# Row exchange for rotary embedding: matrix products replaced by transfers inside SBUF in two of three mixers

## The reference, cut to what matters

```python
def apply_rope(x, cos, sin):
    half = x.shape[-1] // 2
    x1, x2 = x[..., :half], x[..., half:]
    rot = jnp.concatenate([-x2, x1], axis=-1)
    return x * cos + rot * sin
```

## Time and profile before

| | us |
|---|---|
| median of 3 runs | 1736.95 |
| lowest to highest | 1736.74 to 1737.29 |
| the profiled execution, its own time | 1736.61 |
| its span, first to last instruction | 1735.1 |
| TensorE busy in it | 1628.5 |
| VectorE busy in it | 709.8 |
| ScalarE busy in it | 435.5 |

### The profile page before, as it was taken

One profiled execution on the slowest core, in us unless ns is written; L12 is line 12 of the kernel. 1 busy time (PEld: TensorE's weight loads), 2 busy tenths in 40 slices (PEclk: granted clock), 3 DMA queues, 4 the chain that ended last, 5 costly groups with the idle time before them and its releaser, 6 DMA issues.

```text
span 1735.1 us, 22294 instructions
## 1 busy us (share of the span) xinstructions
PE 1628.5 (94%) x9390; PEld 976.6 (56%) x9390; DVE 709.8 (41%) x1379; ACT 435.5 (25%) x770; POOL 32.6 (2%) x39
## 2 busy tenths in 40 slices
PE   7999999999999999999999988988988898889888
PEld 4786999998799999788222322322222223223222
DVE  3677889884787557695111101101101011101102
ACT  3223643435554445453000000000000000000001
POOL 0100000000000000200100000000000000000000
PEclk9999999999999999999999999999999999989999
DMA  9865388848257454329899999999999999999997
GB/s 389 339 243 218 122 322 328 328 164 345 80 207 273 174 215 157 136 98 360 362 415 431 430 431 430 431 431 429 432 430 430 431 430 430 431 431 431 430 430 301
DMA packets 46034, 577.95 MB, mean 333 GB/s; under 512 B 5200, under 2 KB 6256, under 8 KB 9968
## 3 DMA queue, kind: packets, MB, share of 16 engines
q1 hardware_dynamic: 45936, 576.54, 80.6%
HBM read 575.47 MB, written 1.05 MB: 332 GB/s over the span
## 4 chain that ended last, share of the span: by engine, by line
PE 63%; DMA 32%; DVE 2%; ACT 1%; issue 1%; SPq 1%; ACTq 0%; DVEq 0%
DMA RING_T<-in_w_up 29%; PE P L1338 16%; PE P L554 6%; PE P L947 4%; PE P L949 4%; PE P L948 4%; PE P L966 2%; PE P L965 2%; PE P L964 2%; PE P L563 2%; PE P L1365 2%; DMA RING_T<-in_ada_w 1%; DMA RING_T<-in_w_down 1%; PE P L1112 1%; PE P L1114 1%; PE P L1113 1%
## 5 line engine op out<-in xcount | busy, mean ns | idle before, releaser
L1338 PE MATMUL P<-RING_T,SCR 128*34 128x512 f32 x928 | 439.0, 629 | 83.0 <-DMA RING_T<-in_w_up 83.0
L1339 PE MATMUL P<-RING_T,SCR 128*34 128x512 f32 x960 | 453.8, 629 | 0.0
L1338 PEld LDWEIGHTS P<-RING_T,SCR 128*34 128x34 f32 x928 | 104.7, 117 | 366.6 <-issue 365.6
L2874 DVE TENSOR_TENSOR SCR<-P,SCR 34x512 f32<-34x512 f32 x64 | 44.4, 693 | 543.2 <-ACT SCR L2012 543.2
L1365 PE MATMUL P<-RING_T,SCR 128*34 128x512 f32 x480 | 214.6, 595 | 0.4 <-DMA RING_T<-in_w_down 0.4
L1366 PE MATMUL P<-RING_T,SCR 128*34 128x512 f32 x480 | 214.7, 595 | 0.0
L949 PE MATMUL P<-SCF 128*128 128x256 f32 x640 | 181.1, 283 | 0.0
L947 PE MATMUL P<-SCF 128*128 128x256 f32 x640 | 181.1, 283 | 0.0
L948 PE MATMUL P<-SCF 128*128 128x256 f32 x640 | 181.1, 283 | 0.0
L2012 ACT ACTIVATE SCR<-P 34x512 f32<-34x512 f32 x64 | 37.7, 589 | 570.9 <-PE P L1339 570.9
L1365 PEld LDWEIGHTS P<-RING_T,SCR 128*34 128x34 f32 x480 | 49.9, 111 | 135.7 <-issue 130.9
(11 more groups left out here) (430 smaller groups left out, 2438.1 us busy)
## 6 DMA issues: line engine op xcount, KB each, us to landing
RING_T<-in_w_up SPq DMA_DIRECT2D x58, 2048.0 KB, 21.4
RING_T<-in_w_down SPq DMA_DIRECT2D x57, 2048.0 KB, 17.7
RING_T<-in_w_gate SPq DMA_DIRECT2D x56, 2048.0 KB, 18.2
RING_T<-in_ada_w SPq DMA_DIRECT2D x24, 2048.0 KB, 10.4
RING_T<-in_ffn_w SPq DMA_DIRECT2D x22, 2048.0 KB, 8.7
RING_T<-in_ffn_w SPq DMA_DIRECT2D x22, 1024.0 KB, 6.7
RING_T<-in_ab_w_in SPq DMA_DIRECT2D x7, 2048.0 KB, 14.3
RING_T<-in_w_in SPq DMA_DIRECT2D x6, 2048.0 KB, 7.8
```

Source lines behind the costliest of these rows:

```text
L1338: pe.matmul(u.t[0:CAP, :], xs, wg.v(KC, 512)[:, c, :], start=c == 0, stop=c == KC - 1)
L1339: ins = pe.matmul(u.t[64:64 + CAP, :], xs, wu.v(KC, 512)[:, c, :], start=c == 0, stop=c == KC - 1)
```

## The change

In the first and third mixer, the rotation products of all queries, of the indexer's queries and of the third mixer's keys are gone. In their place ScalarE's queue issues transfers from SBUF to SBUF that exchange the row halves into the unused output buffer (`SW`). A head size of 128 takes two transfers, one of 64 takes four. VectorE multiplies the exchanged rows by the sines in place and adds the cosine part. The sign has moved from the matrix to the sines. The first mixer's keys and its index key are still exchanged on TensorE. In all, 44 transfers are added (8 for `iq`, 4 for the queries, 32 in the third mixer). 4 products of 512 columns and 8 of 272 columns are removed, and with them 4 and 8 uses of PSUM banks. The counts that others wait for on `rope` and `drope` are raised, as a rotation by transfer counts twice. Names of semaphores that nothing uses are dropped, too.

```diff
+def act_swap(nc, k, dst, src, rows, sem):
+
+    for z in range(0, 128, 2 * rows):
+        nc.scalar.dma_start(dst[z:z + rows], src[z + rows:z + 2 * rows]).then_inc(k.sem[sem], 16)
+        nc.scalar.dma_start(dst[z + rows:z + 2 * rows], src[z:z + rows]).then_inc(k.sem[sem], 16)
...
+def dve_swapped(nc, k, dst, sw, tmp, sinv, swap, cos_n, cos_sem, sem, n):
+
+    dve, s = nc.vector, k.sem
+    dve.wait_ge(s[swap[0]], swap[1])
+    dve.wait_ge(s[cos_sem], cos_n)
+    dve.tensor_tensor(sw, sw, sinv, ALU.mult).then_inc(s[sem], 1)
+    dve.wait_ge(s[sem], n)
+    dve.tensor_tensor(dst, sw, tmp, ALU.add).then_inc(s[sem], 1)
...
@@ pe_ab
     chunk("gqk", 1)
-    for j in range(4):
-        pe.wait_ge(P["iq", j].taken, P["iq", j].done)
-    pe_rope(nc, k, "rope_iq0", "rot64", v.IQ[:, 0:2, :])
     chunk("gqk", 2)
     chunk("gqk", 3)
-    pe_rope(nc, k, "rope_iq1", "rot64", v.IQ[:, 2:4, :])
...
-    pe.wait_ge(s["norm"], 2)
-    pe_rope(nc, k, "rope_q0", "rot128", v.QA[:, 0:2, :])
-    pe_rope(nc, k, "rope_q1", "rot128", v.QA[:, 2:4, :])
...
-    pe.wait_ge(s["rope"], 7)
+    pe.wait_ge(s["rope"], 11)
@@ pe_diff
-    chunk("k2", 0)
-    rope("q2", v.Q, 0)
-    rope("q2", v.Q, 1)
-    chunk("k2", 1)
-    rope("q2", v.Q, 2)
-    rope("q2", v.Q, 3)
-    for j in (2, 3):
+    for j in range(4):
         chunk("k2", j)
-        rope("k2", v.K, j - 2)
...
     rows(0)
-    rope("k2", v.K, 2)
-    rope("k2", v.K, 3)
     attend(0)
@@ act_ab
     for j in range(1, 4):
         chunk("iq", j, v.IQ[:, j, :])
+    for j in range(2):
+        act.wait_ge(P["iq", j].taken, P["iq", j].done)
+    act_swap(nc, k, v.SW[:, 0:2, :], v.IQ[:, 0:2, :], 32, "swap0")
     u = P["decay"]
     act_out(nc, u, v.BT.rearrange("p a b -> p (a b)"), u.t[:, :])
+    for j in range(2, 4):
+        act.wait_ge(P["iq", j].taken, P["iq", j].done)
+    act_swap(nc, k, v.SW[:, 2:4, :], v.IQ[:, 2:4, :], 32, "swap1")
...
     for z in range(2):
         act.wait_ge(s["norm"], 1 + z)
+        act_swap(nc, k, v.SW[:, 2 * z:2 * z + 2, :], v.QA[:, 2 * z:2 * z + 2, :], 64, f"swap{2 + z}")
         square(v.norms[z], flat(v.KA)[:, 512 * z:512 * z + 512])
@@ act_diff
+    def swap(name, src, n):
+        u = P[name, n % 4]
+        act.wait_ge(u.taken, u.done)
+        act_swap(nc, k, v.SW[:, n, :], src[:, n % 4, :], 32, f"swap{min(n, 6)}")
+
     for j in range(4):
         chunk("q2", j, v.Q[:, j, :])
         split.upto(NSPLIT + j + 1)
+        swap("q2", v.Q, j)
     for j in range(4):
         chunk("k2", j, v.K[:, j, :])
         split.upto(NSPLIT + j + 5)
+        swap("k2", v.K, 4 + j)
@@ dve_ab, and the same for rope_q0 and rope_q1
-    dve_rope(nc, k, "rope_iq0", v.IQ[:, 0:2, :], tmp(0), s64, 1, "rope", "cosm")
-    dve_rope(nc, k, "rope_iq1", v.IQ[:, 2:4, :], tmp(1), s64, 2, "rope", "cosm")
+    dve_swapped(nc, k, v.IQ[:, 0:2, :], v.SW[:, 0:2, :], tmp(0), s64, ("swap0", 64), 1, "cosm", "rope", 1)
+    dve_swapped(nc, k, v.IQ[:, 2:4, :], v.SW[:, 2:4, :], tmp(1), s64, ("swap1", 64), 2, "cosm", "rope", 3)
@@ dve_diff
-        dve.tensor_tensor(src[:, j, :], u.t[:, 0:L], k.SINR, ALU.mult).then_inc(u.taken, 1)
-        dve.wait_ge(u.taken, u.done)
-        dve.tensor_tensor(src[:, j, :], src[:, j, :], tmp, ALU.add).then_inc(s["drope"], 1)
+        dve_swapped(nc, k, src[:, j, :], v.SW[:, n - 1, :], v.bufs[j % 2][:, 0, 0:L], k.SINR, (sem, by), n, "dcos", "drope", 2 * n - 1)
@@ constants
-                m[o + d % n + h, d] = -1.0
+                m[o + d % n + h, d] = 1.0
```

More of the change, by code:

```diff
@@ L132 @@
 UNIT_HIGH, UNIT_LOW = {"ab": 6, "cd": 3}, {"ab": 6, "cd": 4}
+SWAPPED = [("swap0", 128), ("swap1", 128), ("swap2", 96), ("swap3", 96), ("swap4", 64), ("swap5", 64), ("swap6", 128), ("swap6", 128)]
 SQ = {"mix0": 0, "ffn0": 8, "mix1": 16, "ffn1": 24, "mix2": 32, "ffn2": 40}
@@ L269 @@
     "czeros", "cols", "cond", "ada", "mod", "xr", "sa", "square", "squares", "ln", "rs", "lnsq", "hs", "hn",
-    "angle", "trig", "g1one", "iwt", "gate_a", "gate_d", "decay_a", "decay_d", "cosm", "rope", "qeke", "kdqd", "atzero", "at", "relu", "score",
-    "topk", "state", "ot", "nsq", "norm", "logit", "soft", "softmax", "silu_g", "mix",
+    "swap0", "swap1", "swap2", "swap3", "swap4", "swap5", "swap6",
+    "angle", "trig", "g1one", "gate_a", "gate_d", "decay_a", "decay_d", "cosm", "rope", "qeke", "kdqd", "atzero", "score",
+    "topk", "state", "nsq", "norm", "logit", "soft", "softmax", "silu_g", "mix",
     "mixhi", "mixlo", "outhi", "outlo", "rawhi", "rawlo", "rawrow", "hh", "hl", "hi", "lo", "unit", "silu", "hidhi", "hid",
     "xa", "sqb", "uzero", "sabs", "sexp", "lsig", "stick", "pzero", "pool",
-    "split_hi", "split_lo", "dhh", "dhl", "rooted", "rooted_t", "cxs", "lam_d", "lam_a", "dcos", "drope", "amax", "aexp", "asoft", "osq", "osub", "onorm", "czero", "conv",
-    "routed", "sel", "wkzero", "rscaled", "rmax", "rexp", "raff", "rtop", "rmask", "rank", "onehot", "ogzero", "og", "yzero", "esilu", "edown", "fin_in", "fin_sq", "fin_rs", "fin_root", "weighed", "final_d", "final_a",
+    "split_hi", "split_lo", "dhh", "dhl", "rooted", "rooted_t", "cxs", "lam_d", "dcos", "drope", "amax", "asoft", "osq", "osub", "onorm", "czero", "conv",
+    "routed", "sel", "wkzero", "rscaled", "rmax", "rexp", "raff", "rtop", "rmask", "rank", "onehot", "ogzero", "og", "yzero", "esilu", "edown", "fin_in", "fin_rs", "fin_root", "weighed", "final_d", "final_a",
 ]
@@ L405, in __init__ @@
         self.TR = s.take(4, 2 * T)
+        self.SW = self.MIX
         self.COS, self.SIN = s.take(2, T), s.take(2, T)
@@ L773, in score @@
                     ins.then_inc(bb[par].full, 1)
-    pe.wait_ge(s["rope"], 3)
+    pe.wait_ge(s["rope"], 5)
     score(1, 0)
@@ L1153, in attend @@
     def attend(hd):
-        pe.wait_ge(s["drope"], 4 + hd + 1)
+        pe.wait_ge(s["drope"], 2 * (4 + hd + 1))
         for i, (r, m) in enumerate(TILES):
@@ L1580, in square @@
         act.activation(buf[0], src, ACT.Square).then_inc(s["nsq"], 1)
-    act.wait_ge(s["rope"], 2)
+    act.wait_ge(s["rope"], 4)
     act.wait_ge(P["dq", 3].taken, P["dq", 3].done)
@@ L1939, in act_diff @@
     split.upto(19)
-    act.wait_ge(s["drope"], 7)
+    act.wait_ge(s["drope"], 14)
     pv(0)
@@ L1949, in act_diff @@
     split.upto(22)
-    act.wait_ge(s["drope"], 8)
+    act.wait_ge(s["drope"], 16)
     pv(1)
@@ L2442, in dve_ab @@
     select(0, 18)
-    dve_rope(nc, k, "rope_q0", v.QA[:, 0:2, :], v.cos_tmp(0, 0), s128, 4, "rope", "cosm")
-    dve_rope(nc, k, "rope_q1", v.QA[:, 2:4, :], v.cos_tmp(0, 1), s128, 5, "rope", "cosm")
+    dve_swapped(nc, k, v.QA[:, 0:2, :], v.SW[:, 0:2, :], v.cos_tmp(0, 0), s128, ("swap2", 32), 4, "cosm", "rope", 6)
+    dve_swapped(nc, k, v.QA[:, 2:4, :], v.SW[:, 2:4, :], v.cos_tmp(0, 1), s128, ("swap3", 32), 5, "cosm", "rope", 8)
     dve_heads(nc, k, "dk", v.norms, KAf, k.vv("dsa_k"))
@@ L2675, in rope @@
     def rope(name, src, j, n):
[L2676 to L2679, removed]
+        sem, by = SWAPPED[n - 1]
         if n == 1:
             dve.wait_ge(s["rooted"], 2)
-        dve.tensor_tensor(src[:, j, :], u.t[:, 0:L], k.SINR, ALU.mult).then_inc(u.taken, 1)
-        dve.wait_ge(u.taken, u.done)
-        dve.tensor_tensor(src[:, j, :], src[:, j, :], tmp, ALU.add).then_inc(s["drope"], 1)
+        dve_swapped(nc, k, src[:, j, :], v.SW[:, n - 1, :], v.bufs[j % 2][:, 0, 0:L], k.SINR, (sem, by), n, "dcos", "drope", 2 * n - 1)
     def attend(hd):
@@ L3022, in pool_diff @@
             if 4 * n + j >= 2:
-                pool.wait_ge(s["drope"], 4 * n + j - 1)
+                pool.wait_ge(s["drope"], 2 * (4 * n + j - 1))
             pool_cos(nc, k, v.bufs[j % 2][:, 0, 0:L], src[:, j, :], k.COSR, "dcos")
@@ L3242, in constants @@
     inv32 = f(10000.0) ** (-np.arange(32, dtype=f) / f(32))
-    c["inv"] = np.stack([inv64[p % 64], inv32[p % 32]], 1).astype(f)
+    sign = [np.where(p % n < n // 2, f(-1.0), f(1.0)) for n in (128, 64)]
+    c["inv"] = np.stack([sign[0] * inv64[p % 64], sign[1] * inv32[p % 32]], 1).astype(f)
     c["eps"] = np.full((128, 1), EPS, f)
@@ L3249, in constants @@
     ang = np.arange(L, dtype=f)[None, :] * inv32[p % 32][:, None]
-    c["cos2"], c["sin2"] = np.cos(ang).astype(f), np.sin(ang).astype(f)
+    c["cos2"], c["sin2"] = np.cos(ang).astype(f), sign[1][:, None] * np.sin(ang).astype(f)
     c["iota"] = np.broadcast_to(np.arange(1, CAP + 1, dtype=f), (128, CAP))
```

## The result

The kernel with the change takes **1743.96 us**, median of 7 runs (1739.93 to 1745.90), against 1736.80 for the kernel before, measured beside it (7 runs, 1736.71 to 1737.29): ratio 1.0039, 95% interval 1.0029 to 1.0049. It is slower by 7.2 us (0.4%), where 6.7 us less were forecast. In this round its runs lie 6 us apart, those of the kernel before 0.6 us.

What follows compares the result with a forecast made beforehand. TensorE (busy 94%) bounds the kernel until the expert weight stream binds after 830 us. First mixer 3.0 plus third 3.7 gives 6.7 us: 1736.95 - 6.7 = 1730.3 us; forecast's own range 1729.0 to 1731.5, whole range up to 1736.0.

Steps and rivals of the forecast that it cites:

- The sum: Whole kernel: 3.0 us from the first mixer plus 3.7 from the third, 6.7 us gained.
- Removed products: TensorE: 4 products of 0.86 us (3.44) go in the first mixer, 8 of 0.46 (3.7) in the third.
- the free delay of the decay chain: First mixer, ScalarE: indexer transfer issues delay the decay chain by up to 1.8 us, costed at nothing behind other work.
- Landing of the query transfers: First mixer: pairs issued by 127.6 and 131.6 us, wanted at 137.0 and 138.4; 6.8 us left to land.
- Rival 2: First mixer: weight loads delay query transfers, VectorE stands 5.2 us; total gain only 1.5 us, 1735.5 us; chance 0.11.
- Key norm after the change: First mixer: TensorE reaches the second key rotation before VectorE's key norm and waits about 0.4 us.
- Third mixer, price of an issue: ScalarE: four issues at SyncE's price take 1.78 us beside the split unit, so a round takes 2.18 us.
- `rt`, the new wait: Third mixer: second value tile now waits for ScalarE's `rt` copy, out at about 706.1 us; no wait, 5.4 to spare.
- rival 1: Third mixer: ScalarE's issues run in series at SyncE's price, TensorE waits 1.4 us; gain 5.3 us, 1731.7 us; chance 0.14.
- Rival 3: Third mixer: issues at 0.64 us in series, TensorE waits 9.3 us; kernel loses 2.6 us, 1739.6 us; chance 0.08.
- Third mixer, landing: Transfers land in 2.0 us, other end 25.1; the first value tile keeps about 4 us of room.
- VectorE beside GpSimd: VectorE's SBUF operations exclude GpSimd, up to 724 ns; 2.2 us at worst in the third mixer, hidden by TensorE's idle waits.

Runs made afterwards that it cites:

- Indexer alone: Kernel after, but only the indexer's queries rotated by transfer; queries and third mixer stay on TensorE: 1734.91 us (0.9991).
- both new orders and the third mixer's hold: Whole change, key norms before query rotations; third mixer two chunks per transfer, low parts earlier, output weight loads waiting for its transfers: 1729.24 us.
- the loads held: Kernel after with the first mixer's change only; SyncE's second output weight load and all behind it wait for the query transfers: 1733.50 us.
- experiment 7: Kernel after with the first mixer's change only; TensorE multiplies constants ahead of its two waits for key norms: 1738.62 us (1.0014).
- experiment 3: Kernel before, all rotations on TensorE, plus the same 44 transfers copying constants into the unused buffer: 1738.05 us (1.0013).
- experiment 9: First mixer's change only: query chunks in two transfers, 1742.92 us; in eight, 1741.92; one of two weight loads not held back, 1734.55.
- third mixer held: Kernel after with the third mixer's change only; SyncE's two output weight loads wait for all 32 transfers: 1734.46 us (0.9983).
- one load left in place: First mixer's change only; loads behind the last output weight load wait for the query transfers, that 2 MB load does not: 1734.55 us.

## Why the prediction was wrong

- **The sum:** 6.7 us of gain forecast, 7.2 of loss measured. By the traces the first mixer gave -3.55 us for +3.0, the third -2.0 for +3.7. The direction was wrong, and the way this went, slower by more than 3.5 us, had a chance of 0.07.
- **Removed products:** right. The rows named for the clock cover only one of the three pieces, but the windows from 60 to 66 and from 690 to 710 us show 1.00 too. Indexer alone, 1.76 us ahead against 1.72 forecast; the free delay of the decay chain held. With both new orders and the third mixer's hold, 7.4 us were gained, where the products were worth 7.1.
- **Landing of the query transfers:** the step that failed. I took 2.0 us, the output stores, and kept 25.1 us as the other end. The stores go out when nothing else is under way; these transfers go out at the moment at which two weight loads start. The earlier trace rows showed the second of them, at 129.67; the first stands 0.37 us ahead of it. Measured from the first issue to the use were 12.2 us for the first pair, against 9.4 of room (127.6 to 137.0), and 12.3 for the second, whose room of 6.8 us counts from its last issue. VectorE stood 4.7 us.
- **Rival 2** had this mechanism, with 5.2 us, and dismissed it because ScalarE's transfers have a queue of their own. The runs show that a queue of its own does not get them past the loads: 2.3 us with the loads held, 11.7 with them. It read the four loads of the earlier trace rows as going out together; that row is spread over 36.99 us, and two of the loads were under way. It also stopped at the wait: TensorE's clock added 2.2 us in the first mixer (experiment 7 gave 2.0 back), and the sum had no term for it.
- **Key norm after the change, 0.4 us of waiting:** right in size. With the loads held (first mixer alone), 1.91 us ahead at the norm became 3.32 ahead behind the mixer: 0.3 of the second 1.72 us were lost.
- **Third mixer, price of an issue:** mis-sized. 0.37 and 0.47 us apart on SyncE, 0.64 on ScalarE. That an issue runs beside the split unit was right, and by the rule of the Trainium skill, "Perfetto Trace Analysis", "Per-engine timelines", the trace agrees (0.13 us behind its start). What I left out is that the next activation stands behind the issues in ScalarE's queue (1.63 and 1.59 us of waiting, put down to the issues): 2.93 us a round, not 2.18. That this is near my figure for the series (3.03) is chance: there the issues were too cheap and the overlap was missing.
- **`rt`, the new wait:** named rightly, dismissed wrongly. I had it out at 706.1; it is 716.81 + 0.14 - 3.56 = 713.4 us in the time of the kernel before. With transfers landing in 1.9 us the wait was 1.65 us, against 1.4 in rival 1, again by chance, as 1.1 us of it hang on one long issue. Rival 3 had the 0.64 us but in full series, and so a wait of 9.3 us.
- **Third mixer, landing:** 2.0 us taken, "4 us of room". VectorE's longest wait was 5.98 us. Of the 5.7 us lost, issues and bytes alone cost 1.6 (experiment 3); the rest, some 4 us, goes with late landing, and the clock is again in it (0.50 and 0.65 in two windows of 2 us, 1.7 us), which the sum left out here too. The bytes, costed at nothing, take engine time (experiment 9).
- **VectorE beside GpSimd:** the 724 ns are the effect suspected. In the kernel after, a multiply that takes 0.44 us takes 0.91 when it starts inside a GpSimd operation (706.60, with one from 705.70 to 707.22). The Trainium skill, "SBUF — State Buffer", "SBUF: two separate sides", says that the two exclude each other where VectorE has two SBUF inputs, and the trace agrees. It cost nothing that the runs can tell.

## What to carry to other kernels

A small transfer inside SBUF that a waiting engine needs is only as fast as the loads around it allow: look at what the weight queue issues at that moment, and either hold those loads (TensorE used them some 40 us later here) or give the consumer other work first. On ScalarE the next instruction stood until the whole burst of issues was out, and TensorE paid for its waits by its clock, too; so a product removed from the critical engine is worth its time only if nothing new stands before the next one.

## What was not expected of the hardware

- A transfer of 128 KB within SBUF landed in 2.2 to 2.4 us with the loads held, in 6.4 to 10.6 beside one 2 MB load and in 8.5 to 11.8 beside two, though in a queue of its own. The same bytes in half or twice the packets took 9.8 to 12.3 and 8.4 to 12.8 us.
- The 0.5 MB of these transfers kept all 16 DMA engines busy for 2.3 us, a load of 2 MB for 5.3.
- DMA issues on ScalarE's queue are 0.64 us apart, against 0.37 to 0.47 on SyncE's, and single ones took up to 1.74 us.
- After waits of 1.62 and 3.07 us, with one rotation between, TensorE ran at 0.50 for some 4 us more. A single wait of 2.38 us (one load left in place) was followed by the lower clock as well, one of 1.65 us (third mixer held) was not. Constants multiplied in the waits kept it at 1.00 and gave 2.0 us back.
